# Moving the summing of the previous expert's output to the start of each expert's TensorE code

## What is computed

```python
def swiglu(h, w_gate, w_up, w_down):
    return (jax.nn.silu(h @ w_gate) * (h @ w_up)) @ w_down
...
    logits = (xf @ router_w).astype(jnp.float32)
    top_val, top_idx = lax.top_k(logits, TOP_K)
    gates = jax.nn.softmax(top_val, axis=-1)
...
    ys = lax.map(expert_block, (xs, blk_e)).reshape(n_rows, d)
    ys = ys * buf_g[:, None].astype(ys.dtype)
    out = jnp.zeros((n_tok, d), h.dtype).at[buf_tok].add(ys)
```

## Time and profile before

| | busy us | share of the span |
|---|---|---|
| PE | 1508.8 | 91% |
| DVE | 1102.0 | 67% |
| ACT | 962.3 | 58% |
| span of the profiled execution | 1650.3 | |
| time of the profiled execution | 1652.1 | |
| median of 3 runs | 1666.8 | |

### The profile page before, as it was taken

One profiled execution on the slowest core, in us unless ns is written; L12 is line 12 of the kernel. 1 busy time (PEld: TensorE's weight loads), 2 busy tenths in 40 slices (PEclk: granted clock), 3 DMA queues, 4 the chain that ended last, 5 costly groups with the idle time before them and its releaser, 6 DMA issues.

```text
span 1650.3 us, 23029 instructions
## 1 busy us (share of the span) xinstructions
PE 1508.8 (91%) x9225; PEld 1301.8 (79%) x9225; DVE 1102.0 (67%) x1052; ACT 962.3 (58%) x1108; POOL 131.9 (8%) x125
## 2 busy tenths in 40 slices
PE   6989988999979899879999998989898899999986
PEld 6969978999979699779997676666666799866664
DVE  4556545444555565466776888878798676778886
ACT  5356445334353664354445787868778454478776
POOL 6100000000040000001001002020200200100200
PEclk9999998999989999979999999999999999999998
DMA  9318523555633085334667999999999667689993
GB/s 312 113 60 260 184 85 128 179 182 189 200 102 103 25 270 192 115 103 154 230 230 241 322 382 341 377 352 347 385 341 374 232 222 246 236 288 382 354 370 146
DMA packets 224150, 385.79 MB, mean 234 GB/s; under 512 B 11924, under 2 KB 114680, under 8 KB 223880
## 3 DMA queue, kind: packets, MB, share of 16 engines
q1 hardware_dynamic: 223072, 382.12, 66.3%
q10 hardware_dynamic: 424, 1.08, 0.2%
q0 software_dynamic: 512, 0.74, 0.2%
HBM read 382.85 MB, written 1.05 MB: 233 GB/s over the span
## 4 chain that ended last, share of the span: by engine, by line
PE 74%; DVE 12%; ACT 8%; issue 4%; DMA 1%; ACTq 0%; SPq 0%; DVEq 0%
PE banks L1626 12%; PE banks L1627 12%; PE banks L1628 12%; DVE w_low L1152 9%; PE banks L1624 8%; PE banks L1625 7%; PE banks L1937 6%; ACT w_high L730 5%; PE banks L1939 5%; PE banks L1881 2%; PE banks L1873 2%; PE banks L1832 1%; PE banks L1818 1%; DVE after_heads L1424 1%; ACT rows L730 1%
## 5 line engine op out<-in xcount | busy, mean ns | idle before, releaser
L1152 DVE TENSOR_TENSOR w_low<-raw,w_high 128x2048 fp32r<-128x2048 f32 x357 | 808.2, 2292 | 302.7 <-ACT w_high L730 295.9
L730 ACT ACTIVATE w_high<-raw 128x2048 fp32r<-128x2048 f32 x357 | 679.9, 1915 | 279.1 <-PE banks L1939 102.0
L1624 PE MATMUL banks<-w_high,rows 128*128 128x512 f32 (+1 forms) x576 | 224.4, 396 | 30.9 <-DVE w_low L1152 20.9
L1626 PE MATMUL banks<-rows,w_high 128*128 128x256 f32 x832 | 238.3, 286 | 12.2 <-DVE rows L1153 8.6
L1627 PE MATMUL banks<-rows,w_high 128*128 128x256 f32 x832 | 237.6, 286 | 0.0
L1628 PE MATMUL banks<-rows,w_low 128*128 128x256 f32 x832 | 237.4, 285 | 0.0
L1625 PE MATMUL banks<-w_low,rows 128*128 128x512 f32 (+1 forms) x576 | 213.3, 377 | 1.5 <-issue 1.5
L1937 PE MATMUL banks<-rows,w_high 128*128 128x320 f32 x704 | 186.4, 310 | 8.3 <-DVE w_low L1152 5.6
L1939 PE MATMUL banks<-rows,w_low 128*128 128x256 f32 x704 | 184.6, 279 | 0.0
L1626 PEld LDWEIGHTS banks<-rows,w_high 128*128 128x128 f32 x832 | 162.0, 195 | 14.2 <-issue 13.7
L1624 PE MATMUL banks<-w_high,eT 128*128 128x512 f32 x352 | 144.3, 410 | 20.4 <-DVE w_low L1152 13.6
(11 more groups left out here) (200 smaller groups left out, 2028.8 us busy)
## 6 DMA issues: line engine op xcount, KB each, us to landing
raw<-in_moe_w_gate_dram SPq DMA_DIRECT2D x176, 512.0 KB, 5.4
raw<-in_moe_w_up_dram SPq DMA_DIRECT2D x176, 512.0 KB, 5.6
raw<-in_moe_w_down_dram SPq DMA_DIRECT2D x176, 512.0 KB, 5.4
raw<-in_w_in_dram SPq DMA_DIRECT2D x40, 512.0 KB, 6.1
raw<-in_xa_wkv_dram SPq DMA_DIRECT2D x32, 512.0 KB, 8.5
raw<-in_dense_w_gate_dram SPq DMA_DIRECT2D x22, 512.0 KB, 4.4
raw<-in_dense_w_up_dram SPq DMA_DIRECT2D x22, 512.0 KB, 4.2
raw<-in_dense_w_down_dram SPq DMA_DIRECT2D x22, 512.0 KB, 3.6
```

The source lines that it names most:

```text
L730: return act.activation(out_, in_, ACT.Copy, scale=scale)
L1152: return dve.tensor_tensor(out_, in_, plain(high), ALU.subtract)
L1624: pe.matmul(dst, stay[0], move[0], start=start, stop=False, skip_group_check=True)
L1626: pe.matmul(dst, stay[0], move[0], start=start, stop=False, skip_group_check=True)
```

## The change

The calls of `share(e - 1, ...)` in step 0 go, in the wide code and in the narrow code. One call `share(e - 1, range(4))` stands in front of everything else in the expert's code on PE, before the wait for the gathered rows. The code of DVE, ACT, POOL and SP stays as it was.

```diff
                         wide_columns("gate", 0, s)
-                        if e and s == 0:
-                            share(e - 1, (0, 1))
                         wide_columns("up", 1, s)
-                        if e and s == 0:
-                            share(e - 1, (2, 3))
                         if s:
                             outputs(s - 1)
...
+                if e:
+                    share(e - 1, range(4))
                 pe.wait_ge(x_ready, KT * (e + 1))
                 if groups > 2:
                     return wide_expert()
...
                     columns("gate", 0, s)
-                    if e and s == 0:
-                        share(e - 1, (0, 1))
                     if s and blocks == 1:
                         turn(s - 1)
...
                     columns("up", 1, s)
-                    if e and s == 0:
-                        share(e - 1, (2, 3))
                     whole(0, s)
```

## The result

The changed kernel takes 1680.67 us, the median of 4 runs (1678.53 to 1683.58), against 1663.63 us (4 runs) for the kernel before: a ratio of 1.0103, 95% interval 1.0061 to 1.0146, or +17 us. Measured once more on another occasion it was 1681.5 us (6 runs) against 1661.05 us (29 runs), ratio 1.0133 (1.0098 to 1.0169). Forecast were 1683 us and +16 us.

What follows compares the result with a forecast made beforehand. A PE-ACT-DVE loop was taken to pace class 1 experts, PE the wide expert 5. Delays of 12.7 us plus 1.7 and 1.7 for the clock gave 16.1; 1666.8 + 16.1 = 1683 us, range 1671 to 1692.

Steps and rivals of the forecast that it cites:

- The mark: PE's first turn, in step 1 of each class 1 expert: 74.9 us to ACT's output copy, so later turns lengthen the kernel equally.
- From the shares to the turn: Start of class 1 experts: first turn comes 15.99 us after the shares end, through ACT's and DVE's second up piece splits.
- When the shares start: At expert boundaries: shares start 0.28 us after DVE's late copy of y_sb, or after PE's first gate matmul behind wide experts.
- The clock: PE at half clock for 3.4 us after idling costs 1.7 us: once in expert 4, once among experts 2, 3, 7.
- three of five: Of five PE idle times over 2.4 us shown before the change, three were followed by the low clock.
- rival 3: Low clock behind all three new pauses and on the shares of experts 1 and 6: 19.5 to 23 us; chance 0.13.
- Rival 1: Shares disappear in PE's idling at expert boundaries, as DVE's late start sets the turn: −2 to 0 us; chance 0.12.
- Rival 4: Only part of the delay comes through, by shorter DVE or ACT durations or loop catch-up: +5 to +10 us; chance 0.12.
- Rival 2: The share's branches lie open on PE's empty queue at seven boundaries: 7 to 17 us more, 1690 to 1700; chance 0.10.

Runs made afterwards that it cites:

- kept-busy changed kernel: The changed kernel with three float32 matmuls, never read, added on PE at the end of experts 0 to 6: 1674.6 us against 1661.84, ratio 1.0068.
- first-pair kernel: Kernel before with only shares 0 and 1 moved ahead of the first gate columns, 2 and 3 left behind the up columns: 1665.82 us against 1661.84, ratio 1.0025.
- kernel before kept busy: Kernel before with three unread float32 matmuls added on PE at the end of experts 0 to 6: 1657.09 us against 1661.05; again 1655.8 against 1659.98.

## Why the prediction was right, and which terms were off

**The mark.** That a first turn d later makes the kernel d longer held: 75.06 to 75.13 us from turn to copy against 74.9.

**From the shares to the turn.** 16.0 us after the shares' end was forecast. In expert 1 it is 926.75 − (903.75 + 6.84) = 16.16 us, and in expert 2 of the kept-busy changed kernel, at full clock, 1019.35 − (999.78 + 3.42) = 16.15 us. Counted from the row of the first gate matmul it is 16.4 us in all six class 1 experts of the changed kernel (1025.78 − 1009.34 in expert 2), in those of its kept-busy version, and in experts 2 and 3 of the first-pair kernel. The path is the one that was forecast: ACT splits the second up piece when PE's first gate piece ends, and DVE, which had to wait for ACT, is busy from there to the product, as the timelines of ACT and DVE after show in expert 2:

```profile
1011.78 1.92 ACT L730 ACTIVATE w_high<-raw 128x2048 fp32r<-128x2048 f32 x1 [7.58 <-PE banks L1625]
...
1013.73 4.60 DVE L1152 TENSOR_TENSOR w_low<-raw,w_high 128x2048 fp32r<-128x2048 f32 x2 [6.97 <-ACT w_high L730]
...
1025.05 0.68 DVE L1424 TENSOR_TENSOR after_heads<-after_heads,banks 128x512 f32<-128x512 f32 x1
```

This was the core of the forecast. It does not hold everywhere. With the low clock behind a pause the first-pair kernel has 17.9 and 16.7 us in experts 4 and 7, behind the wide experts PE itself comes last there (17.7 us), and where ACT makes both copies it is 16.1 to 17.2 us in experts 2, 3 and 7.

**When the shares start.** 0.28 us behind DVE's copy in experts 2, 3 and 7, so a pause of 3.0 us: right. For expert 1 PE's entry was taken as in before, 2.59 us; it was 2.95. For expert 6 2.55 + 0.28 was taken, and it was 1.69, set by the copy: hence +2.4 instead of +3.4. For expert 4 the pause of 2.48 us in the one profile of before was taken as the entry's length, with DVE's copy as what would come last; it was 5.05 us, and the shares came 2.1 us later than the copy allowed. This is the term that failed most clearly: a single profile cannot give it, as the second profile of before with 4.74 us showed.

**The clock.** One of three new pauses was counted, with 1.7 us, although the prediction's own three of five would have asked for about two. All three had their low clock, in both profiles, and in experts 4 and 5 it lasted 6.8 us instead of the 3.4 taken for expert 4. By its own terms the sum should have been at its upper bound of 19.5 us, which was left to rival 3 with a chance of 0.13. But the stretch in expert 3 was not new, since before had one there too, and neither were the 6.8 us in expert 5; so the share of the clock in the loss is smaller than the number of stretches suggests. The kept-busy kernels bound it. Against the changed kernel's 759.7 us, the same kernel kept busy has 9.6 us less in the experts' time, of which 2.1 us are the entry into expert 4 and part is low clock that before has as well. With both sides kept busy the change costs 16.5 to 18.7 us instead of 23.2 in the experts' time, and 17.5 us by the medians, about the 17 to 20 of the change itself. So the greater part of the loss is the delay of the first turns, and 4.5 to 6.7 us by the profiles, 3 us at most by the medians, are left for the clock and the entries together. No run separates these two. The Trainium skill ("TensorE: Matmul & The Clock Gate", Part 1) says that the clock falls when PE has been idle. The three new pauses agree with that, but the length of a pause does not decide it here: in the first-pair kernel the same pauses of 2.99 us were followed by a clock of 1.00 in experts 2 and 3, and by 0.50 in experts 4 and 7.

**The rivals.** Rival 1, that the shares vanish in the boundary, stays true in part, and the kernel before kept busy shows where it decides: 2 us of delay are free in experts 2, 3 and 7, and 6.4 are not. Rival 3, with 19.5 to 23 us, is nearest to the 23 us of the profiles, but not by its mechanism: the changed kernel has no low clock in experts 1 and 6. Rival 4 falls with the 75.06 and 75.13 us. Rival 2, open branches, did not come about at the first branch, 0.1 to 0.2 us each. But the jump over the two-block copy of the shares took 4.95 us in expert 5 of the changed kernel, by the profile of line 1836 (count, ns min/median/max):

```profile
L1836 PEldq COMPARE_BRANCH  x14: 71/178/4951, 903.5 to 1661.6; - x14
```

It ran beside shares that the low clock had stretched to 6.5 us, and so was hidden; the second profile has 4.39 us there. The Trainium skill ("Runtime: NRT & Kernel Launch", Instruction fetch mechanics) has it that a taken branch stalls when its target lies outside the pages at hand; a median of 0.18 us and single ones of 1 to 5 us agree with that, though no run here moved the code against the pages to show it.

**The total.** The forecast of 1683 us against 1680.7 and 1681.5 owes something to luck. The median of 3 runs from which it started, 1666.8 us, was high, later medians being 1660 to 1664, and the change was set at 16.1 us, where the medians say 17 to 20 and the profiles 23 in the experts. The start was 3 to 6 us too high and the change 1 to 4 us too low, so the two errors cancelled in part. A slip stands in the chances as well: rival 3 has 0.13, and the sum for slower by over 1% takes 0.12.

## What to carry to other kernels

Work that waits for a slow copy does not belong ahead of the instruction whose end starts the next round of the other engines; behind it, the same work can lie in a wait that is there anyway. When a loop of three engines is in balance, look for a mark behind which its length is constant, and count only how the change moves that mark. A new pause of PE can cost twice, once for itself and once for the clock behind it, and both should be in the sum, less what the kernel before already pays. To learn what the clock contributes, keep PE busy in both kernels, not in one. The pauses on entering branched code should be read from more than one profile.

## What the runs showed of the hardware

- In the kernels without added matmuls, entering an expert's code took PE between nothing and 6.1 us of idling, and at the same place of the same program 2.48 and 4.74 us. PE's branch out of expert code (line 484) took 0.42 us in the median and 3.9 to 6.3 us at most in the five such profiles in which it was read; in the changed kernel kept busy it took 0.43 us at most.
- 2.6 us of matmuls whose results nobody reads, put into the pauses of PE, made the changed kernel 4 to 8 us faster by the medians. In the profile the clock is 1.00 behind all pauses but that of expert 5, and the pause on entering expert 4 is gone too, so the gain is not the clock's alone.
- A pause of 2.99 to 3.00 us was followed by the low clock in 8 of 10 cases (experts 2, 3, 7 in both profiles of the changed kernel, 4 and 7 of the first-pair kernel, not its 2 and 3), one of 1.4 or 1.7 us in none of 6. Of the nine pauses of 2.5 to 3.1 us ahead of experts 1 and 6 in the kernels without added matmuls, four were.
- Two profiles of the same program agree within 0.2 us in the experts' time for before (736.5 and 736.4 us) and for the changed kernel (759.7 and 759.9 us), and differ by 2.1 us for before kept busy. The stretch ahead of the experts differs by 8 us between the two of before.
